# Two norms over 512 tokens done in two token halves around the last weight unit before them

## The chip, the cores and the metric

The kernel runs on one core of one Trainium2 chip. Its time is the device time of one execution in microseconds (us); lower is better. The engines are TensorE (PE: matmuls, with its weight loads in rows of their own, PEld), VectorE (DVE), ScalarE (ACT), GpSimd (POOL) and SyncE (SP, which issues the weight loads from memory).

## What is computed

Two layers of a diffusion backbone over 512 tokens of width 1024: 256 context tokens and 256 latent tokens. In layer 0 both halves pass through everything; in layer 1 only the latent tokens are wanted at the end, but the context is still normed and projected to keys and values. Cut to what matters here:

```python
h = rms_norm(x, g_norm1[l]) * (1 + sc1) + sh1
hc = rms_norm(xc, g_norm1[l]) * (1 + scc1) + shc1
y, yc = token_mixer(h, hc, ...)            # input projection, three mixers, merge, w_out
x = x + g1 * y
x = x + g2 * sqrelu_mlp(rms_norm(x, g_norm2[l]) * (1 + sc2) + sh2, w_ff1[l], w_ff2[l])
# the same for xc with its own modulation, where the context is still wanted
```

A norm is over the 1024 features of one token, so the tokens are independent of one another in it. All is fp32 to the outside.

## The kernel before

The stream `x` lies with features on partitions: 8 chunks `c` of 128 features by 512 columns, the context tokens in columns 0 to 255 and the latent ones in 256 to 511. Products are made from split numbers: each operand is cut into a high part that the fast matmul takes exactly and the low rest (`hH` and `hL` for activations, `wH` and `wL` for weights; `oH`, `oL` hold the MLP's hidden values), and each product is three matmuls (high*high, low*high, high*low).

**Weights** come as blocks of 256 output columns (a "unit"). SyncE loads a block into `raw`, ScalarE casts it to `wH` (`high`, L845, two instructions of 1280 and 768 columns), and then GpSimd forms the rest `wL` (`low`, L703 and L705, the same two pieces). Of blocks in the list `SHARED`, which holds the first two units of the input projection (`ml` 0 and 1), the output projection `wo` and others, VectorE does the first piece instead (`share_ahead`, L1294). The buffers hold two such blocks at a time, so block n+2 can be cast only when TensorE is done with block n, and this is written into each engine's program as `ahead(...)`, `low_to(...)` and `share_ahead(...)` at fixed places. Each engine runs its program in order and waits on semaphores.

**A unit on TensorE** is 48 matmuls of 512 columns: for each half `b` of the block's columns, 8 chunks by 3 matmuls into one PSUM bank. VectorE then adds the result to `x` (`residual`, L1813) in the last units of `wo` and of the MLP `ff`, ScalarE squares the new chunks (L894), VectorE adds the squares up (L1803).

**A norm** (the second of layer 0, behind unit `wo` 3, and the first of layer 1, behind unit `ff` 31, are the two changed ones; below "norm 0,1" and "norm 1,0") runs so: when the last unit is done, TensorE sums the squares over the partitions by three matmuls with ones (`squares_total`, L2000 and L2003); ScalarE makes the reciprocal root by Ln and Exp (L906, L907); then per chunk VectorE scales (L1340), ScalarE adds the shift and rounds to `hH` (L915, and L917 for odd chunks), and the low rest is formed by VectorE for even chunks (L1349, semaphore `lowd`) and by GpSimd for odd ones (`norm_low`, L721, semaphore `lowp`). The first units behind the norm (`first_units` with `leading`, L1920) run chunk by chunk as these arrive: three half units at once, so 9 matmuls for each chunk. The fourth half unit (`features`, L1900) follows. Behind norm 0,1 stand the units `ff` 0 and 1; behind norm 1,0 the units `ml` 0 (only the latent columns are needed) and `ml` 1 (all columns).

Each engine's work on the block that reuses the place of the last unit (`ff` 1, or `ml` 1) is done before the scaling: ScalarE's cast between the two last squares, GpSimd's `low` before `norm_low`, VectorE's share after the last residual.

## Time and profile before

| | |
|---|---|
| median of 3 runs | 1616.5 us (1615.98 to 1617.84) |
| time of the profiled execution | 1617.22 us |
| its span, first to last instruction | 1615.5 us |
| TensorE matmul, share of the span | 95% |
| VectorE, ScalarE, GpSimd | 63%, 46%, 43% |

The profiled execution lies 0.7 us above the median, and 1.7 us of its time are outside the span. Matmuls overlap one another, so a row's duration is longer than the time from one start to the next; the latter is what a stream costs. In the profile's rows "x2" with one start means instructions merged into one row, and the square brackets at a row's end give the idle time before it and what ended it. TensorE's granted clock is shown as a share of full speed: 1.00 is 2.4 GHz and 0.50 is 1.2 GHz.

### The profile page before, as it was taken

The page shows a single profiled execution, that of the slowest core. Times are in us where ns is not written, and L with a number is a line of the kernel's source. Part 1 is how long each engine was busy: PE and PEld are TensorE (multiplying, and loading weights), DVE is VectorE, ACT ScalarE, POOL GpSimd, SP SyncE. Part 2 cuts the span into 40 slices and gives each one's busy share as a digit, 9 for nine tenths or more (in the row PEclk, how much of TensorE's full clock was granted, in tenths as well). Part 3 has the DMA queues.
Part 4 walks back from the last instruction along what each step waited for, and adds up shares of the span by engine and source line. Part 5 has one row for each costly group of instructions (what it writes and reads, how often), then busy time and mean ns, then how long its engine had stood idle before and what let it go on. Part 6 is the DMA issues. An engine that isn't in the chain of part 4 may idle for free.

```text
span 1615.5 us, 24884 instructions
## 1 busy us (share of the span) xinstructions
PE 1540.5 (95%) x9666; PEld 1322.1 (82%) x9666; DVE 1019.9 (63%) x1722; ACT 744.6 (46%) x1518; POOL 691.8 (43%) x405
## 2 busy tenths in 40 slices
PE   7899999999999998999999998989998999989998
PEld 3787789877887686788888886988997887989998
DVE  5758936883467764678596957245337387766554
ACT  4425543464545643523223234356436656564442
POOL 0453434724343013455455543565455651234442
PEclk9999999999999999999999999999999999999999
DMA  8453545502144132243454853233421432545553
GB/s 330 183 213 118 179 142 170 186 25 81 61 146 161 31 132 102 75 173 114 182 193 161 298 182 131 72 125 106 141 101 53 153 112 99 183 141 193 183 185 108
DMA packets 69988, 231.17 MB, mean 143 GB/s; under 512 B 18416, under 2 KB 24944, under 8 KB 56560
## 3 DMA queue, kind: packets, MB, share of 16 engines
q1 hardware_dynamic: 60880, 214.19, 37.7%
q10 hardware_dynamic: 8992, 15.39, 2.7%
q8 instruction: 77, 1.26, 0.3%
q14 instruction: 39, 0.32, 0.1%
HBM read 216.98 MB, written 12.58 MB: 142 GB/s over the span
## 4 chain that ended last, share of the span: by engine, by line
PE 74%; DVE 12%; ACT 5%; POOL 4%; issue 4%; DMA 2%; SPq 1%; ACTq 0%; POOLq 0%; DVEq 0%
PE bank L1900 40%; PE bank L1982 9%; PE bank L1938 7%; PE bank L1920 4%; PE bank L1964 3%; PE bank L2293 2%; PE bank L2269 2%; ACT wH L845 2%; PE bank L2280 2%; DVE mjunk L1309 2%; DVE acc L1312 2%; POOL wL L703 1%; PE bank L2143 1%; POOL wL L705 1%; POOL arena L776 1%
## 5 line engine op out<-in xcount | busy, mean ns | idle before, releaser
L845 ACT ACTIVATE wH<-raw 128x768 fp32r<-128x768 f32 (+5 forms) x396 | 298.1, 810 | 395.9 <-PE bank L1900 291.3
L703 POOL TENSOR_TENSOR wL<-raw,wH 128x1280 fp32r<-128x1280 f32 (+2 forms) x143 | 298.1, 2084 | 425.5 <-ACT wH L845 407.1
L705 POOL TENSOR_TENSOR wL<-raw,wH 128x768 fp32r<-128x768 f32 (+3 forms) x198 | 329.6, 1665 | 343.8 <-ACT wH L845 343.7
L1900 PE MATMUL bank<-hH,wH 128*128 128x512 f32 (+1 forms) x720 | 246.8, 343 | 3.2 <-POOL wL L705 1.5
L1900 PE MATMUL bank<-hH,wL 128*128 128x512 f32 (+1 forms) x720 | 244.5, 340 | 0.0
L1900 PE MATMUL bank<-hL,wH 128*128 128x512 f32 (+1 forms) x720 | 244.5, 340 | 0.0
L1900 PE MATMUL bank<-oH,wH 128*128 128x512 f32 (+1 forms) x576 | 193.7, 336 | 0.5 <-issue 0.5
L1900 PE MATMUL bank<-oL,wH 128*128 128x512 f32 (+1 forms) x576 | 193.5, 336 | 0.0
L1900 PE MATMUL bank<-oH,wL 128*128 128x512 f32 (+1 forms) x576 | 193.5, 336 | 0.0
L1312 DVE SCALAR_TENSOR_TENSOR acc<-acc,cb 128x1024 f32<-128x1024 f32 x88 | 165.6, 1895 | 2.5
L1900 PEld LDWEIGHTS bank<-hH,wH 128*128 128x128 f32 x720 | 136.5, 190 | 20.8 <-POOL wL L705 2.1
L1900 PEld LDWEIGHTS bank<-hL,wH 128*128 128x128 f32 x720 | 136.5, 190 | 15.5 <-issue 0.7
L1900 PEld LDWEIGHTS bank<-hH,wL 128*128 128x128 f32 x720 | 136.5, 190 | 15.1
L1982 PE MATMUL bank<-wH,hH 128*128 128x256 f32 x480 | 136.9, 285 | 2.6 <-POOL wL L705 2.1
L1938 PE MATMUL bank<-hH,wH 128*128 128x512 f32 (+1 forms) x384 | 137.0, 357 | 0.8 <-ACT gst L871 0.7
L1982 PE MATMUL bank<-wH,hL 128*128 128x256 f32 x480 | 135.8, 283 | 0.0
L1982 PE MATMUL bank<-wL,hH 128*128 128x256 f32 x480 | 135.8, 283 | 0.0
L1938 PE MATMUL bank<-hH,wL 128*128 128x512 f32 (+1 forms) x384 | 130.9, 341 | 0.0
L1938 PE MATMUL bank<-hL,wH 128*128 128x512 f32 (+1 forms) x384 | 130.8, 341 | 0.0
L1900 PEld LDWEIGHTS bank<-oH,wH 128*128 128x128 f32 x576 | 109.3, 190 | 12.3 <-issue 1.0
L1900 PEld LDWEIGHTS bank<-oH,wL 128*128 128x128 f32 x576 | 109.3, 190 | 11.2
L1900 PEld LDWEIGHTS bank<-oL,wH 128*128 128x128 f32 x576 | 109.3, 190 | 11.1
(214 smaller groups left out, 3046.7 us busy)
## 6 DMA issues: line engine op xcount, KB each, us to landing
raw<-in_p_ff SPq DMA_DIRECT2D x64, 1024.0 KB, 4.8
acc<-in_p_mod SPq DMA_DIRECT2D x44, 1024.0 KB, 5.7
raw<-in_p_ml SPq DMA_DIRECT2D x12, 1024.0 KB, 5.4
...
```

Of the source, the lines that this page charges most:

```text
L703: pool.tensor_tensor(l_[:, 0:cut], r_[:, 0:cut], h_[:, 0:cut].bitcast(F32), ALU.subtract)
L705: pool.tensor_tensor(l_[:, cut:k * w], r_[:, cut:k * w], h_[:, cut:k * w].bitcast(F32), ALU.subtract)\
L845: act.activation(flat(wH, n)[:, part], flat(raw, n)[:, part], ACT.Copy)\
L1309: link(dve.scalar_tensor_tensor(mjunk[:, :], row, 1.0, cb[:, LAT, :], ALU.mult, ALU.mult, accum_out=modT[:, l, chunk, LAT:LAT + 1]))
L1312: ins = dve.scalar_tensor_tensor(row, row, 1.0, cb[:, last, :], ALU.mult, ALU.mult, accum_out=modT[:, l, chunk, last:last + 1])
L1900: ins = pe.matmul(dst, w_[:, kk, c:c + P], r_[:, kk, lo:TOK], start=kk == k0 and m == 0, stop=kk == k0 + kn - 1 and m == 2)
L1920: ins = pe.matmul(dst, w_[:, kk, c:c + P], r_[:, kk, lo:TOK], start=kk == 0 and m == 0, stop=kk == KC - 1 and m == 2)
L1938: ins = pe.matmul(bank[gate_bank(l, T)][:, t0:TOK], w_[:, kk, :], r_[:, kk, t0:TOK], start=kk == 0 and m == 0, stop=kk == KC - 1 and m == 2)
L1964: ins = pe.matmul(bank[2 + T % 2][:, t0:TOK], w_[:, kk, :], r_[:, o + kk, t0:TOK], start=kk == 0 and m == 0, stop=kk == 3 and m == 2)
L1982: ins = pe.matmul(bk[:, o:o + width], s_[:, at[kk], t * P:t * P + P], w_[:, kk, c:c + width], start=kk == 0 and m == 0, stop=kk == k - 1 a ...
L2269: pe.matmul(bank[4 + i][:, 0:nk], l_q[0:MLA_D, 2 * g + i, t * P:t * P + P], l_k[0:MLA_D, 2 * g + i, 0:nk], start=True, stop=True).then_inc ...
L2280: ins = pe.matmul(bank[s % 2][64 * i:64 * i + 64, 0:P], v_[:, c, h * 64:h * 64 + 64], s_pt[:, i, c * P:c * P + P], start=c == 0, stop=c == ...
```

## The change

In the two norms the tokens go by halves, the latent columns (half 0) first and the context columns (half 1) second. The last unit (`wo` 3, `ff` 31) is split by tokens: `last_unit` multiplies both column halves of the block with the latent tokens, then the first with the context tokens into bank 6, then sums the latent squares (`half_total`), then multiplies the last quarter into bank 7. The second sum stands between chunks 1 and 2 of the unit behind the norm. `norm_halves` on ScalarE and VectorE and `norm_low_halves` on GpSimd norm half 0 and then half 1. The unit behind norm 0,1 (`ff` 0) runs its latent columns by chunks as they come, then its context columns, and then `ff` 1 whole. Behind norm 1,0, `ml` 0 (latent columns) runs with half 0 and `ml` 1 (all columns) with half 1. The cast of the block in the last unit's place moves behind chunk 3 of half 1 on ScalarE, its `low` in front of chunk 5 of half 1 on GpSimd, and its share behind chunk 4 of half 1 on VectorE.

```diff
@@ GpSimd
+            def norm_low_halves(l, which, n_end):
+
+                tag = f"nrm{l}{which}_"
+                for h, lo in enumerate((CTX, 0)):
+                    r = slice(lo, lo + 256)
+                    for c in range(1, KC, 2):
+                        if (h, c) == (1, 5):
+                            low_to(n_end)
+                        pool.wait_ge(*S(tag + "high").at(KC * h + c + 1))
+                        pool.tensor_tensor(hL[:, c, r], n_t[:, c % 4, r], hH[:, c, r].bitcast(F32), ALU.subtract)\
+                            .then_inc(S(tag + "lowp").up(1), 1)
+
...
-                low_to(N["ml", l, 2])
-                norm_low(l, 0, 0)
+                if l == 0:
+                    low_to(N["ml", l, 2])
+                    norm_low(l, 0, 0)
+                else:
+                    low_to(reach(N["ff", 0, 30]))
+                    norm_low_halves(l, 0, reach(N["ff", 0, 31]))
...
-                low_to(reach(N["wo", l, 3]))
-                norm_low(l, 1, t0)
-                low_to(N["ml", 1, 0] if l == 0 else N_BLOCKS)
+                if l == 0:
+                    low_to(reach(N["wo", l, 2]))
+                    norm_low_halves(l, 1, reach(N["wo", l, 3]))
+                    low_to(N["ml", 1, 0])
@@ ScalarE
+            def norm_halves(l, which, u, last):
+
+                tag = f"nrm{l}{which}_"
+                sh = M_SH1 if which == 0 else M_SH2
+                halves = [(LAT, slice(CTX, TOK)), (CTXS, slice(0, CTX))]
+
+                def last_square(h, c):
+
+                    r = halves[h][1]
+                    if h == 0:
+                        act.wait_ge(*S(f"bank_free{2 * (u % 2) + c - 6}").at(u // 2 + 1))
+                        act.wait_ge(*S(tag + "add").at(c - 2))
+                    else:
+                        act.wait_ge(*S(tag + "rest").at(c - 5))
+                    act.activation(square_of(c)[:, r], x[:, c, r], ACT.Square).then_inc(S(tag + "sq").up(1), 1)
+
+                def deviation(h):
+
+                    r = halves[h][1]
+                    act.wait_ge(*S(tag + "sum").at(3 * h + 3))
+                    link(act.activation(n_std[:, r], bank[4 + h][:, r], ACT.Ln, scale=1.0 / D, bias=eps[:, 0:1]))
+                    act.activation(n_std[:, r], n_std[:, r], ACT.Exp, scale=-0.5).then_inc(S(tag + "std").up(1), 1)
+
+                def shifted(h, c):
+
+                    s, r = halves[h]
+                    t, bias = n_t[:, c % 4, r], modT[:, l, sh + c, s:s + 1]
+                    act.wait_ge(*S(tag + "t").at(KC * h + c + 1))
+                    ins = act.activation(hH[:, c, r], t, ACT.Identity, bias=bias)
+                    if c % 2:
+                        ins = act.activation(t, t, ACT.Identity, bias=bias)
+                    ins.then_inc(S(tag + "high").up(1), 1)
+
+                last_square(0, 6)
+                last_square(0, 7)
+                if which == 0:
+                    act.dma_start(x_spill[:, :, CTX:], x[:, :, CTX:]).then_inc(S("spilled").handle, 16)
+                last_square(1, 6)
+                deviation(0)
+                for c in range(KC):
+                    shifted(0, c)
+                    if c == 1:
+                        last_square(1, 7)
+                    if c == 3:
+                        deviation(1)
+                for c in range(KC):
+                    shifted(1, c)
+                    if c == 3:
+                        ahead(last)
...
                         exp_and_ln()
+                        if l == 0:
+                            break
                         squares(u0 + 3, l, 1, t0, 6, (0,))
                     ahead(N["wo", l, j])
-                squares(u0 + 3, l, 1, t0, 6, (1,))
-                norm(l, 1, t0)
+                if l == 0:
+                    norm_halves(l, 1, u0 + 3, N["wo", l, 3])
+                else:
+                    squares(u0 + 3, l, 1, t0, 6, (1,))
+                    norm(l, 1, t0)
@@ VectorE
+            def norm_halves(l, which, u, gate, last):
+
+                tag = f"nrm{l}{which}_"
+                sh = M_SH1 if which == 0 else M_SH2
+                halves = ((LAT, slice(CTX, TOK)), (CTXS, slice(0, CTX)))
+
+                def last_residual(h, b):
+
+                    s, r = halves[h]
+                    if h == 0:
+                        src = full(u, b)
+                    else:
+                        dve.wait_ge(*S("half_full").at(2 * (which == 0) + b + 1))
+                        src = bank[6 + b]
+                    ins = dve.scalar_tensor_tensor(x[:, 6 + b, r], src[:, r], modT[:, 0, gate + 6 + b, s:s + 1], x[:, 6 + b, r],
+                                                   ALU.mult, ALU.add)
+                    if h == 0:
+                        free(ins, u, b)
+                    else:
+                        ins.then_inc(S(tag + "rest").up(1), 1)
+
+                def scaled(h, c):
+
+                    s, r = halves[h]
+                    if c >= 4 and c % 2:
+                        dve.wait_ge(*S(tag + "lowp").at(KC // 2 * h + (c - 3) // 2))
+                    dve.scalar_tensor_tensor(n_t[:, c % 4, r], x[:, c, r], gain[:, c, s:s + 1], n_std[:, r],
+                                             ALU.mult, ALU.mult).then_inc(S(tag + "t").up(1), 1)
+
+                last_residual(0, 0)
+                last_residual(0, 1)
+                last_residual(1, 0)
+                for h, (s, r) in enumerate(halves):
+                    dve.wait_ge(*S(tag + "std").at(h + 1))
+                    for c in range(0, KC, 2):
+                        scaled(h, c)
+                        scaled(h, c + 1)
+                        dve.wait_ge(*S(tag + "high").at(KC * h + c + 1))
+                        dve.scalar_tensor_tensor(hL[:, c, r], n_t[:, c % 4, r], modT[:, l, sh + c, s:s + 1],
+                                                 hH[:, c, r].bitcast(F32), ALU.add, ALU.subtract).then_inc(S(tag + "lowd").up(1), 1)
+                        if (h, c) == (0, 0):
+                            last_residual(1, 1)
+                        if (h, c) == (1, 4):
+                            share_ahead(last)
...
+                        if (l, i, j) == (0, 3, 7):
+                            for m in ff_mods(8 * i + j):
+                                mod(m)
+                            break
@@ TensorE
-            def leading(parts, rH, rL, ready):
+            def leading(parts, rH, rL, ready, cols=None, fill=True, between=None):
...
                 for kk in range(KC):
+                    if kk == 2 and between:
+                        between()
...
+            HALVES = (slice(CTX, TOK), slice(0, CTX))
+
+            def half_total(l, which, h):
+
+                tag, r = f"nrm{l}{which}_", HALVES[h]
+                pe.wait_ge(*S(tag + "add").at(KC - 3))
+                pe.matmul(bank[4 + h][:, r], ones, n_sq[:, 0, r], start=True, stop=False).then_inc(S(tag + "sum").up(1), 1)
+                for c in (6, 7):
+                    pe.wait_ge(*S(tag + "sq").at(c + 1 + 2 * h))
+                    pe.matmul(bank[4 + h][:, r], ones, square_of(c)[:, r], start=False, stop=c == 7).then_inc(S(tag + "sum").up(1), 1)
+
+            def half_ready(l, which, h):
+                return lambda kk: S(f"nrm{l}{which}_" + ("lowp" if kk % 2 else "lowd")).at(KC // 2 * h + kk // 2 + 1)
+
+            def last_unit(n, u, l, which, rH, rL):
+
+                H, L = weights(n)
+
+                def product(dst, c, r):
+                    for kk in range(KC):
+                        for m, (w_, r_) in enumerate(((H, rH), (H, rL), (L, rH))):
+                            ins = pe.matmul(dst[:, r], w_[:, kk, c:c + P], r_[:, kk, r],
+                                            start=kk == 0 and m == 0, stop=kk == KC - 1 and m == 2)
+                    return ins
+                for b in range(2):
+                    filled(product(begin(u, b), P * b, HALVES[0]), u, b)
+                product(bank[6], 0, HALVES[1]).then_inc(S("half_full").handle, 1)
+                half_total(l, which, 0)
+                product(bank[7], P, HALVES[1]).then_inc(S("half_full").handle, 1)
...
-                first_units(n0, u0, both(KC, t0), both(KC, 0), hH, hL, lambda kk: low_ready(l, 0, kk))
+                if l == 0:
+                    first_units(n0, u0, both(KC, t0), both(KC, 0), hH, hL, lambda kk: low_ready(l, 0, kk))
+                else:
+                    leading([(n0, u0, b, cut) for b, cut in enumerate(both(KC, t0))], hH, hL, half_ready(l, 0, 0),
+                            between=lambda: half_total(l, 0, 1))
+                    leading([(n0 + 1, u0 + 1, b, cut) for b, cut in enumerate(both(KC, 0))], hH, hL, half_ready(l, 0, 1))
...
+                if l == 0:
+                    last_unit(n0 + 3, u0 + 3, l, 1, hH, hL)
+                else:
+                    features(n0 + 3, u0 + 3, KC, both(KC, t0), hH, hL)
+                    squares_total(l, 1, t0)
...
+                        if (l, i, j) == (0, 0, 0):
+                            lead = [(n, u, b, cut) for b, cut in enumerate(both(KC, t0))]
+                            leading(lead, hH, hL, half_ready(l, 1, 0), HALVES[0], False, lambda: half_total(l, 1, 1))
+                            leading(lead, hH, hL, half_ready(l, 1, 1), HALVES[1])
+                            features(n + 1, u + 1, KC, both(KC, t0), hH, hL)
...
+                        elif (l, i, j) == (0, 3, 7):
+                            last_unit(n, u, 1, 0, oH, oL)
```

On VectorE, around norm 1,0, the instructions before (the last residuals L1813 of unit `ff` 31, the share L1294 of block `ml` 1, and then the norm's scaling L1340 and low parts L1349) stand so:

```order
L1813 SCALAR_TENSOR_TENSOR arena<-bank,modT,arena 128x256 [waits bank_full2]
L1813 SCALAR_TENSOR_TENSOR arena<-bank,modT,arena 128x256
L1813 SCALAR_TENSOR_TENSOR arena<-bank,modT,arena 128x256 [waits bank_full3]
L1813 SCALAR_TENSOR_TENSOR arena<-bank,modT,arena 128x256
L1294 TENSOR_TENSOR wL<-raw,wH 128x1280 [waits w_high]
L1340 SCALAR_TENSOR_TENSOR arena<-arena,gain 128x256 [waits nrm_std]
L1340 SCALAR_TENSOR_TENSOR arena<-arena,gain 128x256 x3
L1349 SCALAR_TENSOR_TENSOR hL<-arena,modT,hH 128x256 [waits nrm_high]
L1349 SCALAR_TENSOR_TENSOR hL<-arena,modT,hH 128x256
```

After the change the second half of the same norm reads so (L1464 is the scaling, L1476 the low part, L1379 the share of block `ml` 1):

```order
L1464 SCALAR_TENSOR_TENSOR arena<-arena,gain 128x256 [waits nrm_std]
L1464 SCALAR_TENSOR_TENSOR arena<-arena,gain 128x256
L1476 SCALAR_TENSOR_TENSOR hL<-arena,modT,hH 128x256 [waits nrm_high]
L1464 SCALAR_TENSOR_TENSOR arena<-arena,gain 128x256 x2
L1476 SCALAR_TENSOR_TENSOR hL<-arena,modT,hH 128x256 [waits nrm_high]
L1464 SCALAR_TENSOR_TENSOR arena<-arena,gain 128x256
L1464 SCALAR_TENSOR_TENSOR arena<-arena,gain 128x256 [waits nrm_lowp]
L1476 SCALAR_TENSOR_TENSOR hL<-arena,modT,hH 128x256 [waits nrm_high]
L1379 TENSOR_TENSOR wL<-raw,wH 128x1280 [waits w_high]
L1464 SCALAR_TENSOR_TENSOR arena<-arena,gain 128x256
L1464 SCALAR_TENSOR_TENSOR arena<-arena,gain 128x256 [waits nrm_lowp]
L1476 SCALAR_TENSOR_TENSOR hL<-arena,modT,hH 128x256 [waits nrm_high]
```

The share of `ml` 1 has moved from in front of the whole norm to behind the fifth chunk of its second half.

On GpSimd, around norm 0,1, before (L703 and L705 are the low part of block `ff` 1, L721 the norm's odd chunks):

```order
L703 TENSOR_TENSOR wL<-raw,wH 128x1280 [waits w_high]
L705 TENSOR_TENSOR wL<-raw,wH 128x768 [waits w_high]
L721 TENSOR_TENSOR hL<-arena,hH 128x512 [waits nrm_high] x4
L703 TENSOR_TENSOR wL<-raw,wH 128x1280 [waits w_high]
L705 TENSOR_TENSOR wL<-raw,wH 128x768 [waits w_high]
```

and after (L709 and L711 are the low parts of the block, first those of `ff` 1 and after the norm those of `ff` 2; L739 are the norm's odd chunks, of 256 columns):

```order
L739 TENSOR_TENSOR hL<-arena,hH 128x256 [waits nrm_high] x6
L709 TENSOR_TENSOR wL<-raw,wH 128x1280 [waits w_high]
L711 TENSOR_TENSOR wL<-raw,wH 128x768 [waits w_high]
L739 TENSOR_TENSOR hL<-arena,hH 128x256 [waits nrm_high] x2
L709 TENSOR_TENSOR wL<-raw,wH 128x1280 [waits w_high]
```

The low part of `ff` 1 has moved from in front of the norm's odd chunks to between the sixth and the seventh of them, that is in front of chunk 5 of half 1.

On TensorE, behind norm 1,0, before (the last sums, L2000 and L2003, and the first matmuls of `leading` for `ml` 0 and 1):

```order
L2000 MATMUL bank<-arena,const 128x512 [waits nrm_add]
L2003 MATMUL bank<-arena,const 128x512 [waits nrm_sq] x2
L1920 MATMUL bank<-hH,wH 128x256 [waits w_share,bank_free1,bank_free2,nrm_lowd,bank_free0]
L1920 MATMUL bank<-hL,wH 128x256
L1920 MATMUL bank<-hH,wL 128x256
```

and after, at the start of unit `ml` 1 (the last matmuls of `ml` 0's chunk 7 and the first of `ml` 1's chunk 0):

```order
L2062 MATMUL bank<-hH,wH 128x256
L2062 MATMUL bank<-hL,wH 128x256
L2062 MATMUL bank<-hH,wL 128x256
L2062 MATMUL bank<-hH,wH 128x512 [waits bank_free3,w_share,nrm_lowd,bank_free2]
L2062 MATMUL bank<-hL,wH 128x512
L2062 MATMUL bank<-hH,wL 128x512
```

Before, the waits on `w_share` for `ml` 0 and `ml` 1 both stood in front of the first chunk of all; now `ml` 1 has one of its own, behind all of `ml` 0.

## Rows read from the trace of the kernel before

**Rows 1.** The page: the first line and the first engine row.
```profile
span 1615.5 us, 24884 instructions
PE 1540.5 (95%) x9666; PEld 1322.1 (82%) x9666; DVE 1019.9 (63%) x1722; ACT 744.6 (46%) x1518; POOL 691.8 (43%) x405
```
**Rows 2.** Stretches: length, then busy time and count of PE, PEld, DVE, ACT, POOL; granted clock, DMA share, GB/s.
```profile
638.50:647.20 8.70, 3.04 (x8) 0.93 (x6) 4.19 (x9) 5.96 (x11) 4.65 (x2) 0.78 0.17 39
999.00:1007.00 8.00, 3.01 (x8) 0.90 (x6) 5.07 (x10) 6.03 (x11) 2.44 (x1) 0.88 0.68 218
```
**Rows 3.** Timeline of TensorE around norm 0,1: start, us, line, operands.
```profile
627.62 0.39 PE L1900 MATMUL bank<-hH,wH 128*128 128x512 f32 x1
...
638.27 0.39 PE L1900 MATMUL bank<-hH,wL 128*128 128x512 f32 x1
638.50 1.02 PE L2000 MATMUL bank<-arena,const 128*128 128x512 f32 x2
639.36 1.02 PE L2003 MATMUL bank<-arena,const 128*128 128x512 f32 x2
...
672.38 0.50 PE L1900 MATMUL bank<-hH,wH 128*128 128x512 f32 x1 [0.99 <-POOL wL L705]
```
**Rows 4.** Timeline of TensorE around norm 1,0.
```profile
988.03 0.39 PE L1900 MATMUL bank<-oH,wH 128*128 128x512 f32 x1
...
1028.66 0.39 PE L1982 MATMUL bank<-wH,hH 128*128 128x256 f32 x1
```
**Rows 5.** Timeline of TensorE in layer 1, matmuls of 256 columns, then the last sum.
```profile
1409.09 0.28 PE L1900 MATMUL bank<-hH,wL 128*128 128x256 f32 x1
...
1413.05 0.28 PE L1900 MATMUL bank<-hH,wL 128*128 128x256 f32 x1
...
1416.10 0.70 PE L2003 MATMUL bank<-arena,const 128*128 128x256 f32 x2 [1.50 <-ACT arena L894]
```
**Rows 6.** The norm of layer 1 that is 256 columns wide: VectorE, ScalarE and GpSimd.
```profile
1417.79 1.08 DVE L1340 SCALAR_TENSOR_TENSOR arena<-arena,gain 128x256 f32<-128x256 f32 x2 [1.26 <-ACT arena L907]
1419.05 0.48 DVE L1349 SCALAR_TENSOR_TENSOR hL<-arena,modT,hH 128x256 fp32r<-128x256 f32 x1 [0.18 <-ACT hH L915]
...
1420.78 0.49 ACT L917 ACTIVATE arena<-arena,modT 128x256 f32<-128x256 f32 x1
...
1424.70 0.73 POOL L721 TENSOR_TENSOR hL<-arena,hH 128x256 fp32r<-128x256 f32 x1 [0.44 <-ACT arena L917]
```
**Rows 7.** Norm 0,1, 512 wide: VectorE's adds and residuals, GpSimd's odd chunks, the wait behind.
```profile
630.44 4.55 DVE L1803 TENSOR_TENSOR arena<-arena 128x512 f32<-128x512 f32 x2 [1.74 <-ACT arena L894]
638.70 0.88 DVE L1813 SCALAR_TENSOR_TENSOR arena<-bank,modT,arena 128x256 f32<-128x256 f32 x2 [2.93 <-PE bank L1900]
647.65 4.91 POOL L721 TENSOR_TENSOR hL<-arena,hH 128x512 fp32r<-128x512 f32 x2 [2.90 <-ACT arena L917]
658.09 1.29 POOL L721 TENSOR_TENSOR hL<-arena,hH 128x512 fp32r<-128x512 f32 x1 [2.11 <-ACT arena L917]
```
**Rows 8.** A block's cast on ScalarE, its low part on GpSimd, a share on VectorE.
```profile
638.76 2.00 ACT L845 ACTIVATE wH<-raw 128x1280 fp32r<-128x1280 f32 x2 [2.32 <-PE bank L1900]
640.11 2.89 POOL L703 TENSOR_TENSOR wL<-raw,wH 128x1280 fp32r<-128x1280 f32 x1 [5.67 <-ACT wH L845]
642.96 1.80 POOL L705 TENSOR_TENSOR wL<-raw,wH 128x768 fp32r<-128x768 f32 x1
1000.55 1.49 DVE L1294 TENSOR_TENSOR wL<-raw,wH 128x1280 fp32r<-128x1280 f32 x1 [0.56 <-ACT wH L845]
```
**Rows 9.** Stretches behind norm 1,0; columns as in rows 2.
```profile
1006.90:1008.00 1.10, 1.09 (x5) 1.10 (x6) 1.10 (x4) 1.10 (x4) 0.60 (x1) 0.50 0.92 387
1014.00:1016.00 2.00, 2.00 (x11) 1.87 (x10) 2.00 (x4) 1.10 (x3) 1.30 (x1) 0.66 0.00 0
```
**Rows 10.** TensorE behind norm 0,1: the clock's low stretch.
```profile
647.16 0.77 PE L1920 MATMUL bank<-hH,wH 128*128 128x512 f32 x1 [4.70 <-DVE hL L1349]
...
649.86 0.52 PE L1920 MATMUL bank<-hH,wH 128*128 128x512 f32 x1
```

55 lines of the change are left out of this document (34 added, 21 removed).

## The prediction

> **What bounds the kernel now.** I read the page first: TensorE is busy 95% of a span of 1615.5 us [rows 1], so a change gains only where TensorE waits. Then the busy time by stretches: behind each of the two last units there is a stretch of 8 to 9 us in which TensorE works only 3 [rows 2], with the clock granted at 0.78 and 0.88, so part of it at the lower level. Last the timeline of TensorE gives a frame for each norm. All times below with a plus are us after the first matmul of the last unit, 627.62 for norm 0,1 and 988.03 for norm 1,0. Before, the third unit from there starts at 672.38 and 1028.66 [rows 3, 4], that is +44.8 and +40.6. These two numbers are what the change has to beat.
>
> A matmul of 512 columns costs 0.227 us from start to start ((638.27-627.62)/47 [rows 3]) and one of 256 costs 0.120 ((1413.05-1409.09)/33 [rows 5]). The matmuls from the frame's start are thus 144 x 0.227 = 32.7 us for norm 0,1 and 96 x 0.227 + 48 x 0.120 = 27.6 for norm 1,0, so 12.1 and 13.0 us are lost there today. That is the most that could be had, 25 us.
>
> **The split unit.** Its first two quarters are 24 matmuls of 256 columns each, 2.9 us, and end at +5.8, the third at +8.7. A sum over 512 columns takes 0.86 us (639.36-638.50 [rows 3]), so I estimate 0.43 for 256. Three of them end at +10.0, the last quarter at +12.8. VectorE is free of the squares' adds at +7.4 (630.44+4.55-627.62 [rows 7]; for norm 1,0 a little earlier), and three half residuals of 0.44 [rows 7] keep it in step. From the last sum's start to the first scaling are 1.7 us (1416.10 to 1417.79 [rows 5, 6]), so the root of half 0 is there at +9.5+1.7 = +11.2. The first chunk follows 1.7 us later (1419.05+0.48-1417.79 [rows 6]) at +12.8, just as TensorE ends the unit. So this part does what it is for.
>
> What is added on TensorE is the price of splitting. Two matmuls of 256 cost 0.240 against 0.227, 13 ns a pair, for 144 pairs (`wo` 3, `ff` 31 and `ff` 0) 1.9 us, and it is inside the times here. The Trainium skill, TensorE: Matmul & The Clock Gate, section Back-to-back issue gap, gives a warm matmul as N/2.4 ns plus 2.5, which would make it 2.5 ns a pair and 0.4 us in all; the trace's 13 ns stands against that, and the sum goes by the trace. The sums (2.6 us a norm) were in the wait before and now lie between products.
>
> **Half 0.** The norm of layer 1 that is 256 columns wide runs from first scaling to last low part in 7.6 us (1417.79 to 1424.70+0.73 [rows 6]), 1.9 us for two chunks. In half 0 there stand between its steps the last context residual (0.44), a square (0.4) and the second root (Ln and Exp, 0.9). With these the half is complete at about +20.6. TensorE, which needs only 5.8 us and one sum for the same chunks, waits for them: `ff` 0's (or `ml` 0's) half ends near +21.7.
>
> This length rests on a hold-up between VectorE and GpSimd. GpSimd's first two odd chunks took 4.91 us together where a later one took 1.29 [rows 7], because VectorE was in its scalings, and the half-wide norm has the same two engines alternate. Half-wide pieces make them alternate twice as often.
>
> **Half 1 of norm 0,1.** ScalarE is through chunk 3 of a half 3.3 us after its first scaling (1420.78+0.49 [rows 6] less 1417.79, less some 0.2 for a first scaling that was late there), at +23.9. Now comes the cast of `ff` 1 (2.00 us) and, 1.35 us behind its start, GpSimd's low part: 640.11 to 644.76, 4.65 us [rows 8]. So GpSimd is held from +25.3 to +30.0, to +31.1 if VectorE's scalings come between its two pieces. Behind it in its queue are the chunks 5 and 7 of half 1, for which TensorE waits: 0.75 us each, with VectorE's chunk 6 between, so chunk 7 is ready at +33.4 and its 6 matmuls end at +34.2. Then `ff` 1 whole, 10.9 us: +45.1. The block behind it, `ff` 2, is no longer late: a cast and low part take 6.0 us (638.76 to 644.76 [rows 8]), ScalarE has two short steps on `ff` 0's result ahead of them, and `ff` 1 now covers 10.9 where only its second half, 5.4, did before. So without the clock +45.1 stands against +44.8: the gain at the front is given back behind GpSimd's queue.
>
> **Half 1 of norm 1,0.** TensorE ends `ml` 0 at +21.7, and then waits for `w_share` of `ml` 1. That share stands on VectorE behind the low part of chunk 4, half 1. The chain is: ScalarE's cast to +25.9, chunk 4 rounded at +26.4; GpSimd is then in the second piece of the block's low part (1.80 [rows 8]) to +27.7, which holds VectorE's low part to +28.1; GpSimd's chunk 5 to +28.9; then the share, 1.49 us [rows 8], to +30.3. TensorE stands 8.6 us. Then `ml` 1 has all chunks at hand or nearly, 48 x 0.227 = 10.9: +41.2, against +40.6 before. Bounds: without any hold-up in this chain the share ends at +28.3; with each alternation 0.2 us dearer at +31.0.
>
> **The clock.** Both norms now have a wait of 6 us or more with little work in it (+26 to +33 with one or two chunks of 0.7 us, and +21.7 to +30.3). Before, behind such a wait the granted clock is 0.50, the lower level of 1.2 GHz. Behind norm 0,1 it held for six matmuls that took 2.70 us for 1.36, a loss of 1.3 (649.86-647.16 [rows 10]); behind norm 1,0 it held from 1006.90 to about 1015.4 (0.66 over 1014 to 1016 [rows 9]), a loss of at most half of 8.5, 4.2 us, some of it hidden in a chunk's wait. These losses are in the +44.8 and +40.6. I take 2.4 for each norm after the change, with 0 and 4.2 as ends.
>
> **The sum.** Norm 0,1: 45.1 + 2.4 - 44.8 = +2.7. Norm 1,0: 41.2 + 2.4 - 40.6 = +3.0. Together 5.7 us slower. ScalarE's issue of the DMA that spills `x` for layer 1 now stands between the latent squares (done at +8.2) and the first context square, which waits for the third quarter at +8.7, so it costs nothing; without that cover it would push the root of half 0 by its own length, under 1 us. No other load or transfer moves. The profiled execution took 1617.22, so it would take 1622.9; from the median of 1616.5 it is **1622.2 us**. The other stretches only shift, and SyncE's load that waits for the later `w_split` of `ff` 1 or `ml` 1 has over 10 us until its cast.
>
> **Rivals.**
> *No change that can be measured* (within 0.2%, 3.2 us, which is about what a measurement of this kernel tells from nothing). The clock stays up in one of the two waits, or comes back quickly: the sum is then 0.9 to 3.2 us, about 1618.5. For it: the loss behind norm 0,1 before was only 1.3 us. Against it: the new waits are as long as the old ones.
> *Faster.* VectorE and GpSimd don't hold each other up on pieces of 256 columns. Then half 0 is complete 1.2 us earlier; in half 1 the pieces of `ff` 1 follow one another, 1.4 us earlier, and the share ends 2.0 us earlier. Norm 0,1 ends 2.6 us before what I say and norm 1,0 3.2, which gives 1616.4; if besides the clock stays up, 4.8 less, 1611.6, and half-way between is the point from which it is a measurable gain. It decides where GpSimd's piece in half 0 takes 0.75 us and not 1 to 1.5. For it: in the narrow norm the later pieces took 0.73 [rows 6]. Against it: the 4.91 us of rows 7. The Trainium skill, GPSIMD Engine Reference, section Key points, says the SBUF interfaces are shared, with contention from VectorE instructions that have two SBUF inputs; by that rule the scalings and low parts do collide and this rival falls, and the 4.91 us agree.
> *Much slower.* The clock stays low for most of the products behind both waits (4.2 each) and every alternation is dearer (0.7 to 1 a norm): 1627.
>
> **How the numbers follow.** My forecast of slower by more than 3.2 us, the last case included, gets 0.62; no measurable change 0.27; faster 0.11. The range leaves out the faster case's far half and the top of the last: 1615 to 1626.5.
>
> **What the profile will show.** Right: TensorE's first chunk matmul behind either norm at about +12.8, the third unit at +45 to +49 and +42 to +46; TensorE's longest wait in norm 1,0 on VectorE's share, 7 to 9 us; in norm 0,1 on GpSimd's chunks 5 or 7, behind its low part of `ff` 1; no wait of `ff` 2. Wrong: a wait of under 4 us before `ml` 1, or chunk 5 of half 1 ready before +30, would show that the front's gain is kept and the kernel faster. A first chunk later than +14 would put the fault into the split unit.

## The result and the profile after

The changed kernel took 1622.89 us (median of 10 runs, 1619.72 to 1625.92) beside 1618.15 us for the kernel before in the same comparison (10 runs, 1615.98 to 1619.92): ratio 1.0029, 95% interval 1.0019 to 1.0038, so 4.7 us slower. The profiled execution took 1621.05 us.

The page of the changed kernel, against [rows 1]:
```profile
span 1619.2 us, 25215 instructions
PE 1543.5 (95%) x9822; PEld 1333.1 (82%) x9822; DVE 1025.4 (63%) x1722; ACT 747.2 (46%) x1526; POOL 689.7 (43%) x413
```
Its busy time by stretches: the two of [rows 2] first, then the waits in half 1 of norm 0,1 and what follows them, then the same for norm 1,0 (columns as there):
```profile
638.50:647.20 8.70, 7.73 (x55) 6.97 (x55) 6.04 (x14) 6.51 (x16) 2.79 (x3) 1.00 0.01 2
999.00:1007.00 8.00, 7.03 (x50) 6.26 (x48) 5.51 (x13) 6.21 (x15) 2.79 (x3) 1.00 0.41 145
650.00:657.50 7.50, 3.48 (x25) 2.99 (x24) 6.38 (x6) 4.16 (x8) 6.75 (x5) 0.97 0.01 2
657.50:661.00 3.50, 3.37 (x17) 3.37 (x18) 0.76 (x2) 0.95 (x4) 0.81 (x2) 0.57 0.91 302
1009.30:1016.90 7.60, 0.04 (x1) 0.02 (x1) 6.26 (x8) 4.35 (x9) 4.24 (x4) 0.68 0.00 0
1016.90:1022.50 5.60, 5.59 (x14) 4.39 (x15) 3.04 (x9) 3.20 (x5) 3.99 (x4) 0.52 0.56 190
```
The holes of before are filled: TensorE works 7.7 and 7.0 us where it worked 3, at full clock. But a new hole stands behind each, and behind the new holes the clock is near 0.5. The timeline of TensorE shows what ends them:
```profile
627.57 0.28 PE L2169 MATMUL bank<-hH,wH 128*128 128x256 f32 x1
...
640.37 0.35 PE L2062 MATMUL bank<-hH,wH 128*128 128x256 f32 x1
...
655.09 0.39 PE L2062 MATMUL bank<-hH,wH 128*128 128x256 f32 x1 [2.38 <-DVE hL L1476]
657.63 0.58 PE L2062 MATMUL bank<-hH,wH 128*128 128x256 f32 x1 [1.56 <-POOL hL L739]
...
693.79 0.39 PE L2040 MATMUL bank<-oH,wH 128*128 128x512 f32 x1
...
987.55 0.28 PE L2169 MATMUL bank<-oH,wH 128*128 128x256 f32 x1
...
1016.91 0.77 PE L2062 MATMUL bank<-hH,wH 128*128 128x512 f32 x1 [7.57 <-DVE wL L1379]
...
1030.44 0.28 PE L2124 MATMUL bank<-wH,hH 128*128 128x256 f32 x1
```
Norm 0,1 has two waits in half 1, for chunk 4 (2.38 us) and chunk 5 (1.56). Norm 1,0 has one of 7.57 us, for VectorE's share of `ml` 1. Here is the work in front of them, first of norm 0,1 (GpSimd, then VectorE, then ScalarE), then of norm 1,0 in order of time:
```profile
651.84 2.92 POOL L709 TENSOR_TENSOR wL<-raw,wH 128x1280 fp32r<-128x1280 f32 x1 [0.32 <-ACT wH L874]
654.70 2.01 POOL L711 TENSOR_TENSOR wL<-raw,wH 128x768 fp32r<-128x768 f32 x1
656.68 0.90 POOL L739 TENSOR_TENSOR hL<-arena,hH 128x256 fp32r<-128x256 f32 x1
658.88 0.73 POOL L739 TENSOR_TENSOR hL<-arena,hH 128x256 fp32r<-128x256 f32 x1 [1.30 <-ACT arena L979]
...
652.93 2.11 DVE L1476 SCALAR_TENSOR_TENSOR hL<-arena,modT,hH 128x256 fp32r<-128x256 f32 x1 [1.12 <-ACT hH L977]
...
650.50 1.99 ACT L874 ACTIVATE wH<-raw 128x1280 fp32r<-128x1280 f32 x2
...
1010.47 1.99 ACT L874 ACTIVATE wH<-raw 128x1280 fp32r<-128x1280 f32 x2
1012.53 1.80 POOL L711 TENSOR_TENSOR wL<-raw,wH 128x768 fp32r<-128x768 f32 x1 [1.07 <-ACT wH L874]
1012.89 1.73 DVE L1476 SCALAR_TENSOR_TENSOR hL<-arena,modT,hH 128x256 fp32r<-128x256 f32 x1 [1.15 <-ACT hH L977]
1014.29 0.91 POOL L739 TENSOR_TENSOR hL<-arena,hH 128x256 fp32r<-128x256 f32 x1
1014.54 2.00 DVE L1379 TENSOR_TENSOR wL<-raw,wH 128x1280 fp32r<-128x1280 f32 x1
```
GpSimd is 4.9 us in `ff` 1's low part before it comes to chunk 5 at +29.1, and VectorE's low part of chunk 4, a piece that takes 0.48 elsewhere, takes 2.11 beside it. That piece also starts late: VectorE was idle for 1.12 us before it, until ScalarE, with the cast of `ff` 1 (1.99 us) in front, had rounded chunk 4. In norm 1,0 the chain is cast, GpSimd's piece, chunk 4, share: the share is done at 1016.5, +29.0.

**Two frames.** To compare executions I use marks that every kernel has: the first product that reads `oH` (`ff` 4, two units behind the third unit of the prediction), and the first product of `ml` 2 (L1982 before, L2124 after). Both are taken from the first matmul of the last unit; where that unit is whole this is the first sum of squares less 10.88 us, as in [rows 3]. Before, `ff` 4 starts here, at +66.65:
```profile
694.27 0.39 PE L1900 MATMUL bank<-oH,wH 128*128 128x512 f32 x1
```
After it is +66.22 and +42.89, against +66.65 and +40.63. So in these two traces norm 0,1 ends 0.4 us earlier and norm 1,0 2.3 us later, which makes 1.8 of the 3.7 us by which the span grew. The other 1.9 lie behind `ml` 2, where both programs are the same but for their line numbers. The stretch from `ml` 2 to the end, of before and of after:
```profile
1028.66:1615.50 586.84, 554.71 (x4424) 521.56 (x4424) 324.52 (x597) 301.69 (x618) 262.05 (x173) 0.98 0.40 135
...
1030.44:1619.20 588.76, 555.82 (x4425) 521.75 (x4423) 325.24 (x597) 301.89 (x618) 262.12 (x173) 0.98 0.40 132
```

### The profile page after: what moved, and what is told of

Same layout as the page of the kernel before. It is cut to its first block, busy times and chain, and to the rows that moved or that the text cites. A ratio compares the mean times of both kernels' runs of the same rounds, so it can differ in the third digit from the quotient of the medians.

```text
span 1619.2 us, 25215 instructions
## 1 busy us (share of the span) xinstructions
PE 1543.5 (95%) x9822; PEld 1333.1 (82%) x9822; DVE 1025.4 (63%) x1722; ACT 747.2 (46%) x1526; POOL 689.7 (43%) x413
## 4 chain that ended last, share of the span: by engine, by line
PE 74%; DVE 12%; ACT 5%; issue 4%; POOL 3%; DMA 2%; ACTq 0%; DVEq 0%
PE bank L2040 39%; PE bank L2124 9%; PE bank L2080 7%; PE bank L2062 4%; PE bank L2106 3%; PE bank L2470 2%; PE bank L2446 2%; ACT wH L874 2%; PE bank L2457 2%; DVE mjunk L1394 2%; DVE acc L1397 2%; POOL wL L709 1%; PE bank L2169 1%; PE bank L2320 1%; POOL wL L711 1%
## 5 line engine op out<-in xcount | busy, mean ns | idle before, releaser
L709 POOL TENSOR_TENSOR wL<-raw,wH 128x1280 fp32r<-128x1280 f32 (+2 forms) x143 | 297.4, 2080 | 421.9 <-ACT wH L874 403.5
L711 POOL TENSOR_TENSOR wL<-raw,wH 128x768 fp32r<-128x768 f32 (+3 forms) x198 | 329.8, 1666 | 337.9 <-ACT wH L874 337.9
L2040 PE MATMUL bank<-hH,wH 128*128 128x512 f32 (+1 forms) x704 | 240.5, 342 | 2.0 <-DVE wL L1379 0.8
L2040 PE MATMUL bank<-hH,wL 128*128 128x512 f32 (+1 forms) x704 | 238.3, 338 | 0.0
L2040 PE MATMUL bank<-hL,wH 128*128 128x512 f32 (+1 forms) x704 | 238.3, 338 | 0.0
L2040 PE MATMUL bank<-oH,wH 128*128 128x256 f32 (+1 forms) x560 | 187.5, 335 | 0.5 <-issue 0.5
L2040 PE MATMUL bank<-oL,wH 128*128 128x256 f32 (+1 forms) x560 | 187.3, 335 | 0.0
L2040 PE MATMUL bank<-oH,wL 128*128 128x256 f32 (+1 forms) x560 | 187.3, 335 | 0.0
L2124 PE MATMUL bank<-wH,hH 128*128 128x256 f32 x480 | 136.7, 285 | 2.9 <-POOL wL L711 2.5
L2080 PE MATMUL bank<-hH,wH 128*128 128x512 f32 (+1 forms) x384 | 137.1, 357 | 0.8 <-ACT gst L900 0.7
L2124 PE MATMUL bank<-wH,hL 128*128 128x256 f32 x480 | 135.8, 283 | 0.0
L2124 PE MATMUL bank<-wL,hH 128*128 128x256 f32 x480 | 135.8, 283 | 0.0
L2080 PE MATMUL bank<-hH,wL 128*128 128x512 f32 (+1 forms) x384 | 131.1, 341 | 0.0
L2080 PE MATMUL bank<-hL,wH 128*128 128x512 f32 (+1 forms) x384 | 130.9, 341 | 0.0
```

What stands on the lines that cost most here:

```text
L709: pool.tensor_tensor(l_[:, 0:cut], r_[:, 0:cut], h_[:, 0:cut].bitcast(F32), ALU.subtract)
L711: pool.tensor_tensor(l_[:, cut:k * w], r_[:, cut:k * w], h_[:, cut:k * w].bitcast(F32), ALU.subtract)\
L2040: ins = pe.matmul(dst, w_[:, kk, c:c + P], r_[:, kk, lo:TOK], start=kk == k0 and m == 0, stop=kk == k0 + kn - 1 and m == 2)
L2080: ins = pe.matmul(bank[gate_bank(l, T)][:, t0:TOK], w_[:, kk, :], r_[:, kk, t0:TOK], start=kk == 0 and m == 0, stop=kk == KC - 1 and m == 2)
L2124: ins = pe.matmul(bk[:, o:o + width], s_[:, at[kk], t * P:t * P + P], w_[:, kk, c:c + width], start=kk == 0 and m == 0, stop=kk == k - 1 a ...
```

## The experiments

Each kernel was timed in five rounds beside the kernel before. The edits stand against the changed kernel unless said otherwise, and are shortened. A difference of 0.001 in the ratio is 1.6 us. This table has the ratios (with 95% interval) and the marks of every profile, in us, which the text below reads:

| kernel | ratio to before | `ff` 4 | `ml` 2 | `ml` 2 to end |
|---|---|---|---|---|
| before | | 66.65 | 40.63 | 586.8 |
| neither | 1.0002 (0.9993 to 1.0011) | 65.82 | 41.02 | 587.4 |
| after | 1.0029 (1.0019 to 1.0038) | 66.22 | 42.89 | 588.8 |
| after2 | 1.0034 (1.0022 to 1.0047) | 66.79 | 41.57 | 587.4 |
| only01 | 1.0018 (1.0008 to 1.0028) | 67.61 | 40.16 | 590.5 |
| only10 | 1.0022 (1.0012 to 1.0033) | 66.78 | 41.77 | 587.8 |
| fill10 | 1.0016 (1.0007 to 1.0025) | 67.64 | 40.25 | 589.3 |
| fill01 | 1.0016 (1.0008 to 1.0025) | 65.64 | 42.85 | 588.6 |
| early10 | 1.0000 (0.9991 to 1.0009) | 67.08 | 37.32 | 588.4 |
| share01 | 1.0004 (0.9995 to 1.0013) | 61.99 | 41.72 | 590.7 |
| late01 | 1.0025 (1.0014 to 1.0036) | 68.02 | 42.77 | 588.3 |
| both | 0.9968 (0.9956 to 0.9981) | 61.96 | 37.30 | 589.3 |
| both2 | 0.9967 (0.9956 to 0.9979) | 61.95 | 38.93 | 588.2 |
| split16 | 1.0062 (1.0051 to 1.0074) | 66.74 | 38.76 | 587.4 |

**only01 and only10: one norm at a time.** Each puts the old code back for one of the two norms on all four engines:
```diff
-def by_halves(l, which):
-    return (l, which) in ((0, 1), (1, 0))
+H01, H10 = True, False      # only10: False, True
...
-                if l == 0:
+                if l == 0 and H01:
                     last_unit(n0 + 3, u0 + 3, l, 1, hH, hL)
```


> Only norm 0,1 goes by halves; norm 1,0 is as in the kernel before. Theory A (the loss sits in norm 1,0, in TensorE's wait for VectorE's share of ml 1 and the low clock behind it): norm 0,1 alone ended at +45.15 against +44.76 in the trace after, so this kernel is 0.4 us slower than the one before, at most 1, ratio 1.0002 to 1.0006. Rival B (the loss is spread over both norms by what the split unit itself costs): half of the 4.7 us, ratio 1.0015.

> Only norm 1,0 goes by halves; norm 0,1 is as in the kernel before. Theory A: nearly the whole loss, +2.3 us at the third unit and up to +4 at the end, ratio 1.0015 to 1.0026. Rival B: half of the 4.7 us, ratio 1.0015, and only01 has the same. If the time beyond the +2.7 us of the two frames comes from layer 1 it stands here and not in only01.

Measured: 1.0018 and 1.0022, about 2.9 and 3.6 us. Theory A fails. Norm 0,1 takes its share of the loss, although the profile after had shown its frame even shorter than before: that execution had the lower clock for only 2.9 us behind the two waits. Three other profiles with the same norm 0,1 (only01, fill10, early10) have it for 5 to 6 us and end 0.9 to 1.4 us later. Rival B's numbers fit, since 1.0015 lies in both intervals, but not its reason: by split16, below, the splitting costs 1.9 us of the 4.7, and share01 and early10 get the loss of a norm back with its unit still split. only01, columns as above:
```profile
657.50:661.00 3.50, 2.46 (x11) 2.46 (x12) 1.66 (x3) 1.42 (x3) 1.72 (x3) 0.52 0.63 215
661.00:664.00 3.00, 3.00 (x13) 2.71 (x12) 1.19 (x2) 1.82 (x3) 0.00 (x0) 0.50 0.24 101
```

**neither and after2: the same programs once more.** neither is only01 with both switches off.

> Neither norm by halves: the program of the kernel before, with its instructions in the same order. It shows how much a second profile and a second set of times differ with nothing changed. Theory: ratio 0.9993 to 1.0007; in the profile both frames as before to 0.5 us, and the stretch from ml 2 to the end longer than the 586.9 us of the first profile by 1 to 3 us, since five profiles of other variants, whose programs are alike from there on, had 587.8 to 590.5. If it is 587 again, the changed kernels lose something in layer 1 that I haven't found.

> The changed kernel again, unaltered, for a second profile. Theory: ratio 1.002 to 1.004; norm 0,1 ends later than in its first profile (ff 4 at about +67.4 instead of +66.2), because three variants with the same norm 0,1 had the low clock for 5 us behind it where the first profile had 2.7; norm 1,0's third unit at +41.8 to +42.9.

Measured: neither 1.0002, so the rearranged source costs nothing that can be measured; after2 1.0034. Neither's frame of norm 0,1 was 0.8 us shorter than before, where I expected 0.5 at most. after2's marks were 66.79 where I expected about 67.4, and 41.57 where I expected 41.8 to 42.9.

The marks vary between profiles of the same norm: `ff` 4 by halves from 66.22 to 67.64, `ml` 2 with the norm whole from 38.76 (split16) to 41.02. So one profile of each can't settle a difference of 2 us, and the mean over the profiles with the same norm is the better figure: norm 0,1 whole 66.50 (4 profiles) and by halves 67.07 (5), norm 1,0 whole 40.14 (4) and by halves 42.26 (6). By the marks the change costs 0.6 and 2.1 us.

The stretch behind `ml` 2, alike in all fourteen profiles, took 586.8 to 590.7 us. In neither it was 587.4, only 0.5 us above before where I expected 1 to 3; my expectation said that this would point to a loss of the changed kernels in layer 1. after2 had 587.4 too, which speaks against it. But taken together the profiles speak for it: the three programs with both norms whole (before, neither, split16) have 586.8, 587.4 and 587.4 (mean 587.2), the eleven others 587.4 to 590.7, in the mean 588.8, which is 1.6 us more. What makes this difference no run shows.

**fill10 and fill01: the clock.** Matmuls into a free bank keep TensorE busy in the waits, and nothing reads them. The edit is fill10's; fill01 has the same helper with 16 and 11 matmuls inside `leading`, ahead of the waits for chunks 4 and 5 of half 1 in norm 0,1:
```diff
+            def busy(n):
+
+                for i in range(n):
+                    pe.matmul(bank[4][:, CTX:TOK], hH[:, 0, CTX:CTX + P], hH[:, 0, CTX:TOK], start=True, stop=True)
...
+                    busy(56)
                     leading([(n0 + 1, u0 + 1, b, cut) for b, cut in enumerate(both(KC, 0))], hH, hL, half_ready(l, 0, 1))
```


> The changed kernel with 56 more matmuls of 256 columns into a bank that nobody reads, between ml 0's half and ml 1's wait for its share: 56 x 0.120 = 6.7 us of the wait of 7.6. Theory A: the granted clock then stays at 1.00 behind the wait, where 12 matmuls took 5.26 us for 2.72, so the third unit starts 2.5 us earlier, at +40.4: ratio 1.0014 against before. Rival C (the low clock there is hidden by the wait for half 1's later chunks, or comes whatever TensorE does): no difference to the changed kernel, 1.0029.

> The changed kernel with 16 and 11 more matmuls of 256 columns into a bank that nobody reads, in TensorE's waits for chunks 4 and 5 of half 1 in norm 0,1 (16 x 0.120 = 1.9 us of 2.38 and 11 x 0.120 = 1.3 us of 1.56). Theory (the clock falls behind these waits in every execution, and for longer in some): the granted clock stays at 1.00, ff 4 starts at +65 to +65.6 instead of +66.2 to +67.6, ratio to before 1.0015 to 1.002, and the times scatter less. Rival (the waits alone make the loss, the clock nothing): 1.003, no change.

Measured: 1.0016 each. In the profiles the granted clock is 1.00 through both places. First fill10 (its wait, then `ml` 1), then fill01's two waits:
```profile
1006.00:1014.00 8.00, 7.10 (x57) 6.69 (x56) 6.39 (x12) 7.09 (x16) 3.72 (x5) 1.00 0.01 2
1014.00:1018.00 4.00, 4.00 (x35) 4.00 (x35) 2.88 (x3) 1.90 (x4) 2.73 (x2) 1.00 0.00 0
1018.00:1022.00 4.00, 3.22 (x16) 2.57 (x15) 2.13 (x4) 2.72 (x5) 1.19 (x2) 1.00 0.49 156
...
655.00:658.00 3.00, 2.49 (x21) 2.28 (x19) 3.00 (x3) 0.14 (x1) 3.00 (x3) 1.00 0.00 0
658.00:661.00 3.00, 2.39 (x18) 1.99 (x17) 1.09 (x2) 1.28 (x3) 1.15 (x2) 1.00 0.83 265
```
`ml` 2 starts at +40.25 where the other profiles have 42.26 in the mean, 2.0 earlier, and `ff` 4 at +65.64 where they have 67.07, 1.4 earlier. By the ratios each fill gives back 0.0013 to 0.0018, 2.1 to 2.9 us, with intervals as wide as that, so the times alone would leave it in doubt. The times also scatter less, as forecast: over 3.6 and 3.7 us in eleven runs each, and over 6.2 us in ten and 6.0 us in five of the changed kernel. The waits themselves end where they did: `ml` 1's first product at +29.3 in fill10 (+29.4 after), held by the same chain of cast, piece, chunk 4 and share, and chunks 4 and 5 at +27.6 and +30.1 in fill01 (+27.5 and +30.1). So theory A and the theory of fill01 stand, and the rivals, which gave the clock no part, fail by the marks, though with one profile each. No run has both fills.

**early10: the work of `ml` 1 moved forward.** The edit is written out here for norm 1,0; norm 0,1 keeps its places.
```diff
@@ ScalarE, in norm 1,0
                 for c in range(KC):
                     shifted(0, c)
+                    if c == 7:
+                        ahead(last)
                 for c in range(KC):
                     shifted(1, c)
-                    if c == 3:
-                        ahead(last)
@@ VectorE
-                        if (h, c) == (1, 4):
+                        if (h, c) == (0, 6):
                             share_ahead(last)
@@ GpSimd: low_to(n_end) before (1, 5) -> behind (1, 7)
```


> The changed kernel with three things placed otherwise in norm 1,0: ScalarE's cast of ml 1 behind half 0's last chunk instead of behind chunk 3 of half 1, VectorE's share of it before half 1's first scaling instead of behind chunk 4, GpSimd's low part of it behind chunk 7 instead of before chunk 5. Theory A (the share's place makes the wait): the share ends at about +23.5 instead of +29.4, ml 1 is then paced by half 1's chunks, no wait of 3 us is left and the clock stays up; third unit at +38 to +39 instead of +42.9, 4 to 5 us less than the changed kernel, ratio to before 1.0000 to 1.0004. Rival D (half 1's chunks set the end, since the cast and the share are now in front of them): third unit at +41 to +43, ratio 1.002 to 1.003.

Measured: 1.0000, third unit at +37.32: theory A's place for this wait stands. The share, the first product of `ml` 1, and the stretch behind it:
```profile
1010.27 1.49 DVE L1387 TENSOR_TENSOR wL<-raw,wH 128x1280 fp32r<-128x1280 f32 x1 [1.34 <-ACT wH L880]
...
1013.37 0.47 PE L2070 MATMUL bank<-hH,wH 128*128 128x512 f32 x1 [2.25 <-DVE hL L1484]
...
1014.00:1018.00 4.00, 4.00 (x13) 3.15 (x12) 3.63 (x8) 3.27 (x9) 2.21 (x3) 0.60 0.01 4
```
A wait of 2.25 us is left, for chunk 0 of half 1 behind the share. The clock did not stay up, which theory A had forecast: the stretch in the last line has 0.60. It cost little, since TensorE has to wait for chunks and for the block behind anyway; both, below, has 1.00 there and reaches `ml` 2 no sooner.

**share01 and late01: `ff` 1's low part.** share01 puts `ff` 1 among the blocks whose first piece VectorE takes, and moves cast, share and GpSimd's piece behind half 1's last chunks; late01 moves them without the sharing.
```diff
-        SHARED = [... or (name, l) == ("ff", 1) for name, l, j in KEYS]
+        SHARED = [... or (name, l) == ("ff", 1) or (name, l, j) == ("ff", 0, 1) for name, l, j in KEYS]
...
@@ norm 0,1: cast behind chunk 7 of half 1, share behind chunk 6, GpSimd's piece behind chunk 7
```


> The changed kernel with norm 0,1 arranged otherwise: VectorE takes the first piece of ff 1's low part (as it does for ml 1), so that GpSimd has only the second; cast, share and GpSimd's piece all stand behind half 1's last chunks. Theory (GpSimd's 4.9 us in ff 1's low part hold up chunks 5 and 7): these chunks come by +29 instead of +32, no wait is over 2 us, the clock stays up, and ff 4 starts at about +63 instead of +66.2 to +67.6: 3 to 4 us less than the changed kernel, ratio to before 1.0003 to 1.001. Rival (half 1's own chain sets the end and the share is now late in its turn): ff 4 at +66 to +67, ratio 1.0025 to 1.003.

> share01 without the sharing: in norm 0,1 the cast of ff 1 and all of its low part on GpSimd stand behind half 1's last chunk, and VectorE takes none of it. It tells whether share01's gain came from the order or from taking 2.9 us off GpSimd. Theory (the work on GpSimd is what counts, the order only moves the wait): half 1 is multiplied by +29 as in share01, then TensorE waits some 4 us for ff 1 (cast 2.0 us from +26.8, low part to about +33), and ff 4 starts at +65.5 to +67: ratio to before 1.002 to 1.003, like the changed kernel. Rival (the order is the gain): ff 4 at +62 to +63 and 1.0004, like share01.

Measured: 1.0004 and 1.0025. Both are through half 1 at +28.5, but then share01 waits 0.69 us and late01 4.30 for the block. share01's TensorE and GpSimd:
```profile
656.68 0.50 PE L2048 MATMUL bank<-hH,wH 128*128 128x512 f32 x1 [0.69 <-DVE wL L1387]
...
653.95 0.74 POOL L744 TENSOR_TENSOR hL<-arena,hH 128x256 fp32r<-128x256 f32 x1 [0.43 <-ACT arena L985]
655.85 2.49 POOL L716 TENSOR_TENSOR wL<-raw,wH 128x768 fp32r<-128x768 f32 x1 [1.16 <-ACT wH L880]
```
late01's:
```profile
660.97 0.80 PE L2048 MATMUL bank<-hH,wH 128*128 128x512 f32 x1 [4.30 <-POOL wL L716]
...
655.79 2.91 POOL L714 TENSOR_TENSOR wL<-raw,wH 128x1280 fp32r<-128x1280 f32 x1 [0.42 <-ACT wH L880]
658.66 2.25 POOL L716 TENSOR_TENSOR wL<-raw,wH 128x768 fp32r<-128x768 f32 x1
```
So the order alone only moves the wait from the chunks to the block; what counts is the 2.9 us piece on GpSimd. late01's `ff` 4 came 1.0 us later than my range, behind a wait at the end of which a 512-column matmul takes 0.80, the sign of the lower clock. Of the 6.0 us between late01's `ff` 4 and share01's, 3.6 are the longer wait; the rest goes with the clock, which fell in late01's wait and stayed at 1.00 through share01's norm 0,1.

**both and both2: a version that beats both kernels.** both is early10 with share01. both2 also has GpSimd's piece of `ml` 1 before chunk 1 of half 1.

> early10 and share01 together. Theory: the gains add, 4 to 5 us in norm 1,0 (seen in early10: third unit at +37.3 instead of +42.9) and 3 to 4 in norm 0,1, so 7 to 9 us less than the changed kernel and 3 to 5 less than the kernel before, ratio 0.997 to 0.998. Rival: only norm 1,0 gives back what it lost, ratio 0.9995 to 1.0005.

> both, with GpSimd's piece of ml 1's low part before chunk 1 of half 1 instead of behind chunk 7. In the profile of both GpSimd waits 3.8 us there, the piece takes 1.8, and TensorE later waits 0.61 us for it and 1.17 for the block behind it. Theory: these two waits shrink, third unit of norm 1,0 at +35.5 to +36.5 instead of +37.3, ratio to before 0.996 to 0.9965. Rival (the piece now holds up VectorE's scalings and chunk 1 itself, which half 1's chain passes on): third unit at +37.3 or later, 0.997 to 0.9975.

Measured: both 1612.20 us (5 runs, before 1617.80), 0.9968: 5.2 us faster than before by the ratio. The two repairs add: `ff` 4 at +61.96 and `ml` 2 at +37.30 are those of share01 and early10 alone. Against the means of the whole norms these are 4.5 and 2.8 us, of which 2.1 are lost again behind `ml` 2 (589.3 against 587.2), and that is the 5.2. both2 is no better (0.9967) and its norm 1,0 ends 1.6 us later: the rival was right on the mark, and the time, between the two forecasts, doesn't tell. VectorE, GpSimd and TensorE at that place in both, and TensorE's first stretch there:
```profile
1007.20 0.87 DVE L1472 SCALAR_TENSOR_TENSOR arena<-arena,gain 128x256 f32<-128x256 f32 x2
...
1014.60 1.85 POOL L716 TENSOR_TENSOR wL<-raw,wH 128x768 fp32r<-128x768 f32 x1
...
1008.88 0.47 PE L2070 MATMUL bank<-hH,wH 128*128 128x512 f32 x1 [2.26 <-DVE hL L1484]
...
1008.00:1014.00 6.00, 5.12 (x22) 4.22 (x23) 5.20 (x11) 5.12 (x13) 2.75 (x4) 1.00 0.01 3
```
and in both2, with TensorE's first stretch behind the wait:
```profile
1006.16 2.42 DVE L1472 SCALAR_TENSOR_TENSOR arena<-arena,gain 128x256 f32<-128x256 f32 x2
...
1005.46 2.44 POOL L716 TENSOR_TENSOR wL<-raw,wH 128x768 fp32r<-128x768 f32 x1 [1.16 <-ACT wH L880]
...
1009.39 0.76 PE L2070 MATMUL bank<-hH,wH 128*128 128x512 f32 x1 [3.79 <-DVE hL L1484]
...
1009.40:1014.00 4.60, 4.60 (x11) 3.63 (x12) 4.23 (x9) 3.73 (x10) 2.61 (x3) 0.50 0.53 215
```
The piece fills a gap of GpSimd's own, but it runs beside VectorE's share and first two scalings: it takes 2.44 instead of 1.85 and the scalings 2.42 instead of 0.87. The wait grows from 2.26 to 3.79 us, and at this length the clock falls behind it.

**split16: the price of splitting.** The kernel before, with 16 units in the middle of `ff` 0 multiplied by token halves:
```diff
+                        parts = ((0, CTX), (CTX, TOK)) if l == 0 and i in (1, 2) else ((0, TOK),)
...
-                    dst = begin(u, b)[:, lo:TOK]
-                    for kk in range(k0, k0 + kn):
+                    dst = begin(u, b)
+                    for p0, p1 in parts:
+                        p0 = max(p0, lo)
+                        for kk in range(k0, k0 + kn):
...
```


> The kernel before with one thing changed: 16 units of ff 0's middle part (i = 1 and 2) are multiplied by token halves like the last unit, so that 768 matmuls of 512 columns become 1536 of 256, with no wait near them. The price of splitting alone. By the 13 ns a pair of the sum: 768 x 0.013 = 10.0 us, ratio 1.0062. If a pair costs nothing, 1.000, and the 1.9 us for the split in the sum fall away. The Trainium skill, TensorE: Matmul & The Clock Gate, section Back-to-back issue gap, would give 2.5 ns a pair, 1.9 us.

Measured: 1.0062, 10.0 us for 768 pairs, 13 ns each. The trace gives the same: from `ff` 4 to the first matmul of `ff` 31 it took 304.01 us, and 293.76 in every other profile, 10.25 more. The same 60 us of before and of split16:
```profile
740.00:800.00 60.00, 60.00 (x266) 49.67 (x266) 36.55 (x33) 19.49 (x27) 32.15 (x12) 1.00 0.35 123
...
740.00:800.00 60.00, 60.00 (x503) 60.00 (x502) 33.37 (x31) 20.00 (x27) 29.01 (x11) 1.00 0.34 124
```

## Why the prediction was right, point by point

**Sign and size.** 5.7 us slower was forecast and 4.7 measured. The likeliest case came about by the mechanism forecast: the front's gain is lost in half 1 of each norm. The number is closer than its parts, and that is luck. By the marks the two norms lose 0.6 and 2.1 us where I had 2.7 and 3.0, and some 1.6 us lie behind `ml` 2, where the sum had nothing ("the other stretches only shift"). The parts were these.

**The front.** Right: the first chunk matmul stands at +12.80, half 0 is complete at about +20.6, and the clock is up. One row was misread on the way: 1416.10 in [rows 5] is the start of two sums merged, so the 1.7 us to the first scaling are not from the last one. It did no harm: VectorE's first scaling came at +11.1, where I had +11.2.

**The split.** 13 ns a pair was right (split16). The Trainium skill's 2.5 ns (TensorE: Matmul & The Clock Gate, section Back-to-back issue gap) is not what this stream pays. The section gives that formula for an isolated matmul, and says that in a stream with a weight load for each matmul both set the spacing; the loads of split16, busy 60.00 of 60 us, agree with that.

**Half 1 of norm 0,1.** The mechanism was right and its size 1.4 us too large: GpSimd began `ff` 1's low part at +24.3 instead of +25.3, and chunk 7 was ready at +32.0 instead of +33.4. With the clock held up (fill01) `ff` 4 starts at +65.64. Less the 21.8 us of two units (96 x 0.227) that is +43.8 for the third unit, where I had +45.1 without the clock. The forecast of TensorE's longest wait there was half right: it is VectorE's chunk 4, behind the cast and beside GpSimd's piece, and chunk 5 is second. No wait of `ff` 2 is left, as forecast.

**Half 1 of norm 1,0.** Right in mechanism: the wait for the share took 7.57 us (8.6 forecast) and ended at +29.4 (+30.3). With the clock up (fill10) `ml` 2 starts at +40.25, where I had +41.2. early10 shows that this order was the cause.

**The clock.** The term was 2.4 us for each norm. The profiles say 1.4 and 2.0, the ratios of fill01 and fill10 2.1 to 2.9. So its size was about right, but what I had not weighed is that it differs from one execution to the next, and that [rows 9, 10] were one draw of it. The changed kernel's ten runs show it: the six with spans of 1620.7 to 1624.1 us have a mean granted clock of 0.982 or 0.983, the four of 1617.9 to 1619.3 us 0.984 or 0.985.

**What stays open.** The marks of the profiles give 0.6 + 2.1 = 2.7 us, the times 4.7 and 5.5 (lower ends of the intervals 3.1 and 3.6). The 1.6 us behind `ml` 2 would bring the marks to 4.3, but they rest on three profiles against eleven, and their cause is not known. Both profiled executions of the changed kernel were also quicker than its median, by 1.8 and 4.0 us. only01 and only10 add up to 6.5 us, more than both norms together cost, but within their intervals.

**The rivals.** The faster case rested on VectorE and GpSimd not holding each other up. The sign I had named, GpSimd's pieces in half 0 at 0.75 us or at 1 to 1.5, came out between the two: 0.74, 1.03, 1.03 and 0.84 in both norms, this the second of norm 0,1:
```profile
643.00 1.03 POOL L739 TENSOR_TENSOR hL<-arena,hH 128x256 fp32r<-128x256 f32 x1 [1.70 <-ACT arena L979]
```
What decided was half 1, where the pieces are larger, and there the case fell: VectorE's 2.11 and 1.73 us for a piece of 0.48 stand in the profile after, and both2's pair of rows is the clearest case. The shared SBUF interfaces of the Trainium skill (GPSIMD Engine Reference, section Key points) agree with it. The much slower case did not come, since the two losses of 4.2 didn't fall together.
